# Splitting one more weight half of the next expert before an expert's results are read out of PSUM

## The reference

```
def _swiglu(x, w_gu, w_down):
    g, u = jnp.split(x @ w_gu, 2, axis=-1)
    return (jax.nn.silu(g) * u) @ w_down

def _moe(x, w_router, w_exp_gu, w_exp_down):
    logits = (x @ w_router).astype(jnp.float32)
    top_v, top_i = lax.top_k(logits, TOP_K)
    gates = jax.nn.softmax(top_v, axis=-1)
    gate = jnp.sum(jax.nn.one_hot(top_i, N_EXPERTS, dtype=jnp.float32) * gates[..., None], axis=-2)
    out = jnp.zeros_like(x)
    for e in range(N_EXPERTS):
        out = out + _swiglu(x, w_exp_gu[e], w_exp_down[e]) * gate[..., e:e + 1].astype(x.dtype)
    return out
```

## Time and profile before

| | us |
|---|---|
| median of 3 runs | 1769.95 |
| the runs | 1770.01, 1769.95, 1766.35 |
| the profiled execution, time | 1765.79 |
| its span | 1764.0 |
| mean granted TensorE clock, share of full speed | 0.985 |

### The profile page before, as it was taken

How to read it: one execution, slowest core, us unless ns; L and a number is a source line. 1 busy time by engine, 2 the same in 40 slices (tenths; PEclk the granted TensorE clock), 3 DMA queues, 4 the chain that set the end, 5 groups by cost and what they waited for, 6 DMA issues and landing times.

```text
span 1764.0 us, 22681 instructions
## 1 busy us (share of the span) xinstructions
PE 1696.8 (96%) x8446; PEld 1319.4 (75%) x8446; DVE 1183.1 (67%) x1522; ACT 824.0 (47%) x853; POOL 142.8 (8%) x138
## 2 busy tenths in 40 slices
PE   7999999999999999999999999999999999999993
PEld 4645487689999664648767888888888888888883
DVE  2687535354543367663524798988888888888895
ACT  1122211144442212221112677777777778777772
POOL 0530000000000063000003200000000000000000
PEclk9999999999999999999998999999999999999997
DMA  9656553855534535655385689999999999999992
GB/s 319 199 204 215 214 197 109 294 186 175 179 132 144 181 122 204 217 218 191 139 302 182 213 301 366 394 361 390 364 388 375 376 378 376 387 373 382 373 397 64
DMA packets 220720, 466.71 MB, mean 265 GB/s; under 512 B 11150, under 2 KB 50248, under 8 KB 220630
## 3 DMA queue, kind: packets, MB, share of 16 engines
q1 hardware_dynamic: 213446, 444.76, 69.6%
q0 software_dynamic: 4896, 16.77, 3.4%
q10 hardware_dynamic: 2304, 4.20, 0.6%
HBM read 447.10 MB, written 18.74 MB: 264 GB/s over the span
## 4 chain that ended last, share of the span: by engine, by line
PE 85%; DVE 7%; ACT 3%; issue 2%; DMA 2%; SPq 1%; ACTq 0%; DVEq 0%; POOLq 0%
PE bank L1227 83%; PE bank L1231 3%; DVE arena L2674 1%; DVE ring_low L2154 1%; ACT high L1778 1%; DMA out<-mem_rows 1%; DVE R L2288 0%; DMA y_rows<-arena,slot_row 0%; ACT arena L1842 0%; DVE st L2646 0%; DVE st L2567 0%; ACT SQ L1863 0%; SPq L730 0%; SPq L736 0%; DVE pair_in L2307 0%
## 5 line engine op out<-in xcount | busy, mean ns | idle before, releaser
L2154 DVE TENSOR_TENSOR ring_low<-ring,high 128x2048 fp32r<-128x2048 f32 x264 | 600.7, 2291 | 88.6 <-ACT high L1778 87.6
L1778 ACT ACTIVATE high<-ring 128x2048 fp32r<-128x2048 f32 x264 | 505.5, 1919 | 136.6 <-PE bank L1227 127.6
L1227 PE MATMUL bank<-high,xg_high 128*128 128x512 f32 x704 | 278.9, 396 | 4.4 <-DVE ring_low L2154 4.4
L1227 PE MATMUL bank<-ring_low,xg_high 128*128 128x512 f32 x704 | 275.1, 391 | 0.0
L1227 PE MATMUL bank<-high,xg_low 128*128 128x512 f32 x704 | 275.0, 391 | 0.0
L1227 PEld LDWEIGHTS bank<-high,xg_high 128*128 128x128 f32 x704 | 132.6, 188 | 34.9 <-DVE ring_low L2154 8.5
L1227 PEld LDWEIGHTS bank<-ring_low,xg_high 128*128 128x128 f32 x704 | 132.6, 188 | 28.3
L1227 PEld LDWEIGHTS bank<-high,xg_low 128*128 128x128 f32 x704 | 132.7, 189 | 26.3
L1842 ACT ACTIVATE arena<-bank 128x512 f32<-128x512 f32 (+3 forms) x89 | 43.1, 521 | 210.9 <-PE bank L1227 141.4
L1227 PE MATMUL bank<-high,he_high 128*128 128x512 f32 x352 | 139.1, 395 | 0.0
L1227 PE MATMUL bank<-ring_low,he_high 128*128 128x512 f32 x352 | 137.2, 390 | 0.0
(11 more groups left out here) (321 smaller groups left out, 2424.3 us busy)
## 6 DMA issues: line engine op xcount, KB each, us to landing
ring<-in_w_exp_gu SPq DMA_DIRECT2D x176, 1024.0 KB, 13.8
ring<-in_w_exp_down SPq DMA_DIRECT2D x40, 2048.0 KB, 15.8
ring<-in_w_in SPq DMA_DIRECT2D x12, 2048.0 KB, 11.6
ring<-in_w_ffn_gu SPq DMA_DIRECT2D x22, 1024.0 KB, 8.6
ring<-in_w_ckv SPq DMA_DIRECT2D x8, 2048.0 KB, 8.2
ring<-in_cache_mem_k SPq DMA_DIRECT2D x16, 1024.0 KB, 8.2
ring<-in_cache_mem_v SPq DMA_DIRECT2D x16, 1024.0 KB, 6.8
ring<-in_cache_attn_k SPq DMA_DIRECT2D x32, 256.0 KB, 4.2
```

The costliest lines, as they stand in the source:

```text
L1227: return M.matmul(out, lhsT, rhs, start=start, stop=stop)
L1778: S.activation(high_bufs[h % HIGH_BUFS][:], ring[:, s, j * HALF:(j + 1) * HALF], ACT.Copy).then_inc(split_high, 1)
L2154: V.tensor_tensor(ring_low[:, s, part], ring[:, s, part], high_bufs[h % HIGH_BUFS][:], ALU.subtract).then_inc(split_low, 1)
```

## The change

`low_part` takes a fourth argument that says which halves of the chunk it does. In the body of an expert, chunk 1 is now done with its second half only. The first half of chunk 1 (half 2) moves in front: for the first expert of a pass to just before the loop, behind the slot tables (`slots`), and for every later expert into the conditional block in front of the readout of the expert before. There it stands behind halves 0 and 1, and ahead of the waits for `dn_done` and `y_rows_written` and of the two readout instructions. Nothing is added or taken away on any engine; PE's, ACT's, POOL's and SP's lists are the same.

```
--- before.py
+++ after.py
@@ -2147,8 +2147,10 @@
                                     X_BANKS[n][:, 0:4 * lots].rearrange("p (k n) -> p k n", k=4),
                                     xg_high[:, 4 * n:4 * n + 4, 0:lots], ALU.subtract).then_inc(xg_low_ready, 1)
 
-            def low_part(e, c, p):
+            def low_part(e, c, p, which=(0, 1)):
                 for j, h in halves_of(p):
+                    if j not in which:
+                        continue
                     dve.wait_ge(split_high, expert_no(e, c) * HALVES + (h + 1))
                     s, part = epos[p][2], slice(j * HALF, (j + 1) * HALF)
                     V.tensor_tensor(ring_low[:, s, part], ring[:, s, part], high_bufs[h % HIGH_BUFS][:],
@@ -2175,7 +2177,7 @@
                                     he_high[:, 4 * q:4 * q + n, 0:lots], ALU.subtract).then_inc(T_low, 1)
 
                 for p in range(1, NGU + NDN):
-                    low_part(e, c, p)
+                    low_part(e, c, p, (1,) if p == 1 else (0, 1))
                     if 2 <= p <= NGU and (p % 2 == 0 or p == NGU):
                         multiply((p - 1) // 2)
                     for q in range(PAIRS):
@@ -2185,6 +2187,7 @@
 
                 with dve.If(e < EXPERTS - 1):
                     low_part(e + 1, c, 0)
+                    low_part(e + 1, c, 1, (0,))
                 dve.wait_ge(dn_done, i * NDN + NDN)
                 dve.wait_ge(y_rows_written, rows_written(e, c))
                 for n in range(2):
@@ -2220,6 +2223,7 @@
                 low_part(0, c, 0)
                 low_of_gathered((2 * EXPERTS + 2) * c, x_groups_before(0, c) - 2)
                 slots(c)
+                low_part(0, c, 1, (0,))
                 with dve.Fori(0, EXPERTS) as e:
                     expert(e, c)
```

## The result

| | before | changed |
|---|---|---|
| median of 22 runs, us | 1767.31 | 1771.41 |
| lowest and highest | 1764.94, 1775.79 | 1768.99, 1780.72 |
| profiled execution, time and span | 1765.79, 1764.0 | 1769.23, 1767.3 |
| mean granted clock | 0.985 | 0.986 |

The ratio is 1.0028, with a 95% interval of 1.0015 to 1.0041: the change makes the kernel slower by 0.28%, some 5.0 us; the medians lie 4.1 apart. The forecast was +5.4 us, 0.3%. The median of before moved from the 1769.95 of three runs to 1767.31 with 19 more.

A forecast was written before the change was run, and what follows sets the result against it. PE was taken to bound the kernel, stopping at each change of expert. Seven changes x 0.77 us gave +5.4 us: 1769.95 + 5.4 = 1775.3 us, range 1770.0 to 1779.0.

The forecast's parts named there:

- Low part 2 starts no earlier: At each change of expert, DVE's low part 2 still waits for ACT's high part 2, starting at 1080.57 again: gain 0.
- The readout pushes low part 3 by 1.32 us: On DVE between low parts 2 and 3: 0.66 us uncovered plus 0.11 restart, a 0.77 us PE stop per change; chance 0.77.
- POOL's 0.09, taken as 0: Low part 2 ran 0.09 us longer beside POOL's scatter; this moves to low part 3 or 4, bounds -0.09 to +0.09 per change.
- The branches stay hidden: DVE's sequencer does its branches behind the start of low part 2, which runs 2.3 us: cost 0, otherwise up to 0.66 per change.
- No third stop, and DVE catches up: Low part 4 starts 0.3 us late, ends near 1088.7 before PE wants half 4 at 1089.33; DVE has its lateness back.
- The rule of the Trainium skill: Next DVE instruction issues only once the pipe has emptied: low part 3 some 0.24 us later, sum about 7.1 us.
- Faster: Rival: the readout held low part 2, so PE's first stop shrinks; -0.6 us, or -5.7 for a real gain; chance 0.03.
- taken back: Rival: PE's second stop shortens a later wait in the same expert; 0 to -0.6 us; chance 0.09 (taken back or covered).
- branches uncovered: Rival: DVE's branches at a change of expert are not hidden; up to 7 x 1.43 = 10.0 us, 1780.0; chance 0.07.
- The clock: Rival: PE's second stop lowers the granted clock, 1.04 us per drop, 7.3 on top of the 5.4, 1782.6; chance 0.04.
- The table load ahead of high part 2: At a change of expert ACT loads a table (1.28 us), since the SiLU comes next in its loop.
- The level: Starting time for the +5.4 us: median 1769.95 giving 1775.3, or profiled execution 1765.79 giving 1771.2.

The follow-up runs named there:

- the doses: Readout between low parts 2 and 3 for 0.66, 1.32, 2.07 and 3.06 us (half, changed kernel, 8 pieces, 16 pieces): periods 94.35, 95.00, 95.74 and 96.74 us.
- the fourth experiment: Changed kernel, with ACT also making high part 2 ahead of its branch back: ratio to the kernel before 1.0002, median 1768.08 us, period 94.09 us.
- experiments 1 and 3 to 7: Ratios to before: readout halved around low part 2 (1.0010); readout behind low part 3 (1.0014); high part 2 early (1.0002), readout first (0.9993); both with later SiLU (0.9953, 0.9976).

## Why the prediction was right, point by point

- *Low part 2 starts no earlier.* Right. DVE's idle time ahead of it went from 0.82 to 2.13 us, and it began at 1079.70, 0.02 behind the end of high part 2 at 1077.75 + 1.93 = 1079.68.
- *The readout pushes low part 3 by 1.32 us, of which 0.66 is covered; with the restart 0.77 us.* Right: 0.77 measured, and the doses show a slope of 1 above a cover of about 0.66.
- *POOL's 0.09, taken as 0.* This is the term that was off. Low part 2 took 2.29 us with the scatter no longer beside it (before it took 2.37 at the first change and 2.33 at the next ones, as in the line below), and no later low part took longer (2.28), so it was won and not paid back: 0.77 - 0.04 = 0.73 per change, 5.1 in all and not 5.4.

```profile
1174.88 2.33 DVE L2154 TENSOR_TENSOR ring_low<-ring,high 128x2048 fp32r<-128x2048 f32 x1 [0.80 <-ACT high L1778]
```

- *The branches stay hidden.* Right: the readout starts at 1081.91, 0.08 ahead of the end of low part 2. There is no gap that a branch could fill, and at the second change the branches were done at 1175.33, 1.66 us before low part 2 ended.
- *No third stop, and DVE catches up.* Right: the waits are 14. Low parts 3, 4 and 5 ran without a gap, and at 1093.29 DVE was waiting for ACT again (0.42 us).
- *The rule of the Trainium skill (VectorE: DVE Perf Modes, The DRAIN you can't avoid)* as the prediction took it would have given 7.1 us. The same section goes on to say that a next instruction that is not held starts earlier, which the prediction left out. The trace agrees with that addition: low part 2 ended at 1079.70 + 2.29 = 1081.99 and the readout started at 1081.91, and the step to low part 3 overlaps by 0.08 us too.
- *Faster, taken back, branches uncovered:* none occurred. *The clock* stayed at 1.00 with stops of 0.77 and 1.25 us, and fell with 2.25; that rival had the right mechanism for a longer stop than the change makes, and its price of 1.04 us per drop was low: some 1.5 were measured.
- *The table load ahead of high part 2.* The prediction gave the SiLU as its reason. That does not fit: another load stands directly ahead of the SiLU (L1790, 1.28 us at 1081.48 in the changed kernel), and from the first change on the trace of before has seven of each. No number of the sum hung on the reason, but the second load is what the fourth experiment ran into.
- *The level.* I put the +5.4 on the median of three runs and got 1775.3; with 22 runs the level is 1767.31, and 1771.41 is nearer to what the same sum gave from the profiled execution, 1771.2. The step from span to median was the weak one, and cost nothing only because the range held both levels.

## What to carry to other kernels

Work that sits in the idle time of an engine that waits for another one is free. A reorder that puts the waiting instruction first doesn't start it earlier; it moves the free work behind it, where only the slack of the next consumer covers it. Compare two numbers before such a move: when the operand is ready, and how long after its own result the next one is needed (here 0.66 us, against 1.32 of work). And when a stop is removed, follow every engine at least one buffer turn further: the second table load and the SiLU were hidden only by PE's first stop.

## What the runs showed of the hardware that I had not expected

- The clock fell behind a stop of 2.25 us in five of seven changes of expert, and matmuls took 0.63 us instead of 0.39 for some 3 us. Behind 1.25 us it did not in any.
- POOL's issue of the scatter took 1.58 to 1.64 us where it began within 0.05 us of a low part (before), 2.85 where it began 0.9 us into one (the changed kernel and experiments 1 and 3 to 7), and 7.26 in both kernels with the readout in pieces. In the 2.85 case, end less 1.58 falls at the end of the running low part (1084.17 + 2.85 - 1.58 = 1085.44, low part 3 ended near 1085.5). The Trainium skill (SBUF — State Buffer, Who interferes with whom) says that a `tensor_tensor` with both inputs in SBUF contends with GpSimd's reads, and infers that descriptor generation is not held up by it; what I see looks like a hold. The 7.26 fits a hold until the third low part in a row has ended: with 8 pieces, at the second change, 1181.06 + 7.26 - 1.58 = 1186.74, and low part 5 ended at 1180.18 + 6.68 = 1186.86. Why it is three there and one in the changed kernel is open. Nothing waited for the scatter.
- A DVE instruction out of PSUM costs some 0.125 us besides its columns when many follow each other. For the same 1024 columns, 16 instructions took 3.06 us, 8 took 2.07 and 2 took 1.32: (3.06 - 2.07) / 8 = 0.124, (2.07 - 1.32) / 6 = 0.125.
